# Turning x, y and seven heads' probabilities by transposing transfers in a two-block decoder kernel

## The reference, cut to what matters

```python
proj = rms_norm(h) @ w_in            # z, xbc, dt, q, k, v, two gates
xbc = silu(causal_depthwise_conv(xbc, conv_w, conv_b))
x, B, C = split(xbc)                 # x: 32 heads of 64, in 4 groups of 512 columns
# for each group: scores C.B * decay, applied to x*dt; state = B^T (x*dt*decay); y_off = C.state * decay
y = (y_diag + y_off + d_skip * x) * silu(z)
y = y * rsqrt(mean(y*y per group)) * ssd_norm
p = softmax over three dilated windows of q.k     # 8 heads
o = p @ v
merged = sigmoid(g_ssd) * (y @ w_ssd) + sigmoid(g_attn) * (o @ w_attn)
h = h + merged @ w_out ; h = h + (silu(gate) * up) @ w_down
```

## Time and profile before

| what | value |
|---|---|
| median of 3 runs | 1545.76 us (1545.64 to 1547.02) |
| the profiled execution's own time | 1546.51 us |
| its span, first to last instruction | 1544.7 us |
| busy: PE, DVE, ACT, POOL | 99%, 66%, 60%, 5% |
| granted TensorE clock, mean of the span | 1.000 |
| DMA queue of SP | 276.44 MB, 53.8% of 16 engines |

### The profile page before, as it was taken

How to read it: one execution, slowest core, us unless ns; L and a number is a source line. 1 busy time by engine, 2 the same in 40 slices (tenths; PEclk the granted TensorE clock), 3 DMA queues, 4 the chain that set the end, 5 groups by cost and what they waited for, 6 DMA issues and landing times.

```text
span 1544.7 us, 19149 instructions
## 1 busy us (share of the span) xinstructions
PE 1526.3 (99%) x7734; PEld 1288.4 (83%) x7734; DVE 1021.0 (66%) x1324; ACT 924.0 (60%) x1114; POOL 79.1 (5%) x55
## 2 busy tenths in 40 slices
PE   7999999999999999999999999999999999999998
PEld 7888888888888888988888888888888878888887
DVE  5978776646665554787886665566555576677665
ACT  5766777474355553667677566436555465656564
POOL 1000000000001000000000000000110020002000
PEclk9999999999999999999999999999999999999999
DMA  7455554554457675445555464446767575437541
GB/s 272 165 172 156 178 167 174 168 181 156 148 210 222 204 217 199 164 159 163 171 178 170 169 173 170 163 165 207 216 189 235 211 250 187 149 137 244 178 148 71
DMA packets 100399, 280.09 MB, mean 181 GB/s; under 512 B 65079, under 2 KB 66008, under 8 KB 69848
## 3 DMA queue, kind: packets, MB, share of 16 engines
q1 hardware_dynamic: 99208, 276.44, 53.8%
q10 hardware_dynamic: 1104, 2.43, 0.4%
HBM read 261.69 MB, written 1.84 MB: 171 GB/s over the span
## 4 chain that ended last, share of the span: by engine, by line
PE 86%; DVE 6%; ACT 4%; issue 3%; DMA 0%; ACTq 0%; DVEq 0%
PE ps L641 23%; PE ps L643 23%; PE ps L642 23%; PE ps L646 3%; DVE w_low L1640 2%; PE ps L911 2%; PE ps L912 2%; PE ps L913 2%; ACT w_high L1154 2%; PE ps L774 2%; DVE conv L1726 1%; DVE scratch L1931 1%; PE ps L818 1%; PE ps L749 0%; PE ps L779 0%
## 5 line engine op out<-in xcount | busy, mean ns | idle before, releaser
L1640 DVE TENSOR_TENSOR w_low<-w_raw,w_high 128x2048 fp32r<-128x2048 f32 (+1 forms) x250 | 566.7, 2267 | 410.1 <-ACT w_high L1154 343.3
L641 PE MATMUL ps<-w_high,u_high 128*128 128x512 f32 x1376 | 547.6, 398 | 0.5 <-DVE w_low L1640 0.5
L1154 ACT ACTIVATE w_high<-w_raw 128x2048 fp32r<-128x2048 f32 (+1 forms) x196 | 369.2, 1884 | 288.7 <-PE ps L643 275.3
L643 PE MATMUL ps<-w_high,u_low 128*128 128x512 f32 x1376 | 536.9, 390 | 0.0
L642 PE MATMUL ps<-w_low,u_high 128*128 128x512 f32 x1376 | 536.1, 390 | 0.0
L643 PEld LDWEIGHTS ps<-w_high,u_low 128*128 128x128 f32 x1376 | 258.2, 188 | 55.1
L641 PEld LDWEIGHTS ps<-w_high,u_high 128*128 128x128 f32 x1376 | 258.6, 188 | 54.6 <-issue 1.9
L642 PEld LDWEIGHTS ps<-w_low,u_high 128*128 128x128 f32 x1376 | 258.7, 188 | 53.0 <-issue 1.9
L641 PE MATMUL ps<-w_high,b_high 128*128 128x512 f32 x384 | 152.2, 396 | 0.0
L643 PE MATMUL ps<-w_high,b_low 128*128 128x512 f32 x384 | 149.8, 390 | 0.0
L642 PE MATMUL ps<-w_low,b_high 128*128 128x512 f32 x384 | 149.6, 390 | 0.0
(11 more groups left out here) (236 smaller groups left out, 1430.8 us busy)
## 6 DMA issues: line engine op xcount, KB each, us to landing
w_raw<-in_stream SPq DMA_DIRECT2D x238, 1024.0 KB, 4.9
w_raw<-in_stream SPq DMA_DIRECT2D x12, 512.0 KB, 4.1
par<-in_pars SPq DMA_DIRECT2D x4, 269.0 KB, 5.2
h<-in_x SPq DMA_DIRECT2D x4, 256.0 KB, 5.1
ple_gain<-in_ple_g ACTq DMA_DIRECT2D x2, 512.0 KB, 5.2
out<-h SPq DMA_DIRECT2D x4, 256.0 KB, 2.0
scratch<-in_const SPq DMA_DIRECT2D x1, 768.0 KB, 7.4
rev<-scratch ACTq DMA_DIRECT2D x1, 768.0 KB, 3.6
```

The lines of the kernel that those rows point to most:

```text
L641: nc.tensor.matmul(o, hi, whi, start=start, stop=False, **kw)
L643: return nc.tensor.matmul(o, lo, whi, start=False, stop=stop, **kw)
L1154: nc.scalar.activation(WH[:, c % RING, 0:n], W[:, c % RING, 0:n], ACT.Copy).then_inc(high_ready, 1)
L1640: return nc.vector.tensor_tensor(out=o, in0=a, in1=b, op=op)
```

## The change

x of each group, y of each group and the probabilities of heads 0 to 6 are no longer turned by PE. POOL splits the words, SP issues a transposing DMA and POOL (for q and k still ACT) puts them together. In each first-block layer this takes away 32 turns of x, 32 of y and 21 of probabilities, and adds 15 transposing DMAs on SP and some 30 copies on POOL. Slots move: DVE takes x in 2i+9 (was 2i+7), now from `xdt` in SBUF, y first, then `xds`, then `xdt` in place; the state's product moves from PE 2i+7 to 2i+8, behind the rows of that slot; ACT's copy of the state from 2i+8 to 2i+10; y is weighed in 2i+19 for groups 0 to 2 and 2i+16 for group 3 (was 2i+15); the product with v comes in s+4 (was s+3), its halves in s+6, its bank is 7 in place of 6; `QK_MERGE` of q2 goes from 30 to 31. SP's order within a slot is load, `turn_x`, `turn_qk`, `turn_y`, `turn_p`, rows.

```diff
+        X_TURN, QK_TURN, Y_TURN = (0, 2, 5, 8), (1, 4, 7, 10, 12, 13, 14), (3, 6, 9, 11)
+        QK_MERGE = (14, 24, 31, 34, 46, 47, 48)
+        X_AT = 9
+        Y_WEIGH = (19, 19, 19, 16)
+        O_AT = tuple(s + 6 - (s == 54) for s in HEAD_AT)
@@ SP
+            def turn_x(l, c):
+                for g, i in enumerate(XT):
+                    m = X_TURN[g]
+                    if c == 2 * i + 9:
+                        sp.wait_ge(words_split.sem, words_split.at(l, m + 1))
+                        sp.dma_start_transpose(x_back.rearrange("p (m r) -> p m r", r=P), ...)
+            def turn_y(l, c):          # c == 2 * i + 16
+            def turn_p(l, c):          # c == s + 6, heads 0 to 6
                     load(l * CHUNKS1 + c, c % RING, l * BLOCKS1 + c, 0, CH)
+                    turn_x(l, c)
                     turn_qk(l, c)
+                    turn_y(l, c)
+                    turn_p(l, c)
...
                     for g, i in enumerate(XT):
                         for t in range(T):
                             if c == (13 if g == 0 else 2 * i + 6 + 2 * t):
                                 load_rows(l, g, t)
@@ PE
-                    if c == 2 * i + 5:
-                        ... eight turns of conv
-                    if c == 2 * i + 13:
-                        ... eight turns of Y[g % 2]
-                    if c == 2 * i + 7:
-                        pe.wait_ge(xds_ready.sem, xds_ready.at(l, g + 1))
+                    if c == 2 * i + 8:
+                        pe.wait_ge(x_ready.sem, x_ready.at(l, 2 * g + 1))
...
+                        nc.tensor.matmul(ps[:, 5, :], btok[:, g, :], xds, start=True, stop=True).then_inc(state_ps.sem, 1)
+                    if n < 7 and c == s + 4:
+                        pe.wait_ge(pt_out.sem, pt_out.at(l, n + 1))
+                        if n == 6:
+                            pe.wait_ge(att_masked.sem, att_masked.at(l, 8))
+                        elif n:
+                            pe.wait_ge(o_ready.sem, o_ready.at(l, n))
+                        weigh_values(n)
@@ ACT
+                        if c == 2 * i + 10:
+                            ... copy of the state from ps[:, 5, :]
-                        if c == 2 * i + 15:
+                        if c == 2 * i + Y_WEIGH[g]:
                             for t in range(T):
                                 act.wait_ge(y_weighted.sem, y_weighted.at(l, 2 * g + t + 1))
...
@@ POOL, in this order
+                for g in range(GROUPS):
+                    split_x(g)
+                    if g:
+                        split_y(g - 1)
+                    else:
+                        split_qk(0)
+                    merge_x(g)
+                    if g:
+                        merge_y(g - 1)
+                        split_qk(g)
+                split_y(3)
+                merge_y(3)
+                ... lay_apart(n) and put_together(n) for heads 0 to 6, between them split_qk(4) to (6)
@@ DVE
+                        if c == 2 * i + X_AT:
+                            dve.wait_ge(x_whole.sem, x_whole.at(l, g + 1))
...
+                            tt(heads(xds), heads(xdt[:, 0, :]), ...).then_inc(x_ready.sem, 1)
+                        if c == 2 * i + Y_WEIGH[g]:
+                            dve.wait_ge(y_whole.sem, y_whole.at(l, g + 1))
```

More of the change, by code:

```diff
@@ L675, in ffn_turn, with weigh_values @@
                 last.then_inc(ffn_cols.sem, 1)
+            def weigh_values(n):
+                b, v = O_BANK[n], vv[n // 4][:, :, tok(n % 4)]
+                nc.tensor.matmul(ps[:, b, 0:S], v[:, 0], pT[:, 0:S], start=True, stop=False)
+                nc.tensor.matmul(ps[:, b, P:S], v[:, 1], pT[:, S:S + P], start=False, stop=True).then_inc(o_ps.sem, 1)
             def before(l, c):
@@ L751, in before @@
                             last.then_inc(row_ps.sem, 1)
-                    if c == 2 * i + 7:
-                        pe.wait_ge(xds_ready.sem, xds_ready.at(l, g + 1))
-                        pe.wait_ge(ssd_exp.sem, ssd_exp.at(l, 2 * g + 1))
-                        nc.tensor.matmul(ps[:, 6, :], btok[:, g, :], xds, start=True, stop=True).then_inc(state_ps.sem, 1)
-                for g, i in enumerate(XT):
-                    if c == 2 * i + 13:
-                        pe.wait_ge(y_scaled.sem, y_scaled.at(l, g + 1))
-                        if g < GROUPS - 1:
-                            pe.wait_ge(xdt_ready.sem, xdt_ready.at(l, g + 2))
-                        else:
[L762 to L766, removed]
+                    if c == 2 * i + 8:
+                        pe.wait_ge(x_ready.sem, x_ready.at(l, 2 * g + 1))
+                        if g == 0:
+                            pe.wait_ge(btok_out.sem, btok_out.at(l, 1))
+                            pe.wait_ge(cumt_out.sem, cumt_out.at(l, 1))
+                        else:
+                            pe.wait_ge(ssd_y.sem, ssd_y.at(l, 2 * g))
+                        nc.tensor.matmul(ps[:, 5, :], btok[:, g, :], xds, start=True, stop=True).then_inc(state_ps.sem, 1)
                 for g, i in enumerate(XT):
@@ new lines, in put_together, with split_x @@
+                def put_together(n):
+                    pool.wait_ge(p_turned.sem, p_turned.at(l, 16 * (n + 1)))
+                    if n:
+                        pool.wait_ge(o_ps.sem, o_ps.at(l, n))
+                    nc.gpsimd.tensor_copy(pT.bitcast(U16).rearrange("p (n h) -> p h n", h=2),
+                                          p_back[n // 4][:, :, :].rearrange("p (h k) n -> p h (k n)", h=2)).then_inc(pt_out.sem, 1)
+                def split_x(g):
+                    pool.wait_ge(conv_act.sem, conv_act.at(l, 3 + g))
+                    for t in range(T):
+                        ins = nc.gpsimd.tensor_copy(x_half[:, :, t], conv[:, :, tok(t)].bitcast(U16).rearrange("p j (n h) -> p h j n", h=2))
+                    ins.then_inc(words_split.sem, 1)
@@ L1877, in _ @@
                                 chain.then(dve, tt(dt_out, dt[:, 0:HEADS], dec_out, ALU.mult))
-                            tt(heads(xds), heads(ps[:, 4, :]), bc(dt_out[:, g * HPG:(g + 1) * HPG].unsqueeze(2), HPG, HD), ALU.mult)\
-                                .then_inc(xds_ready.sem, 1)
+                            for t in range(T):
+                                tt(heads(y[:, t, :]), heads(xdt[:, t, :]),
+                                   bc(par[:, C_DS + g * HPG:C_DS + (g + 1) * HPG].unsqueeze(2), HPG, HD), ALU.mult)
+                            tt(heads(xds), heads(xdt[:, 0, :]), bc(dt_out[:, g * HPG:(g + 1) * HPG].unsqueeze(2), HPG, HD), ALU.mult)\
+                                .then_inc(x_ready.sem, 1)
+                            for t in range(T):
+                                ins = tt(heads(xdt[:, t, :]), heads(xdt[:, t, :]),
+                                         bc(dt[:, t * HEADS + g * HPG:t * HEADS + (g + 1) * HPG].unsqueeze(2), HPG, HD), ALU.mult)
+                            ins.then_inc(x_ready.sem, 1)
                         for t, at_c in ((0, 2 * i + 8), (1, 2 * i + 10)):
```

192 lines of the change are left out of this document (121 added, 71 removed).

## The result

The changed kernel takes 1570.68 us (median of 4 runs, 1568.84 to 1571.85) against 1545.70 in the same session: ratio 1.0158, interval 1.0146 to 1.0170, **25 us slower where 12 were forecast** and 0.7 above the end of the range.

The account below looks back on a forecast made before the run. PE, busy 1526.3 of 1544.7 us, was taken to bound the kernel. Per layer -13.1 + 3.0 + 6.2 + 4.5 + 0.3 + 0.9 + 1.7 + 2.5 = +6.0, two +12.0 on 1545.8: 1558, range 1546 to 1570.

Parts of the forecast that it names:

- turns and waits for `pT` gone: On PE: turns of x, y and probabilities and seven waits for turned probabilities disappear; 13.1 us less a layer.
- New wait 1, rows: PE waits for group 0's rows, issued behind `turn_x` in SP's slot 13; 3.0 us a layer.
- New wait 2, group 2 (with `merge_y`): PE's state product waits for `xds` in slot 24: 6.2 us, plus 0.9 for `split_low` beside `merge_y`.
- New wait 2, group 3: PE's state product waits for `xds`, with y's weighing in slot 29 ahead of it; 4.5 us a layer.
- New wait 2, groups 0 and 1: PE's state product waits for `xds` with no weighing before it; 0.3 us for both groups.
- New wait 3, slot 47: PE's turns of q5 wait for bank 7 until head 3's halves are made in slot 48; 1.7 us a layer.
- Clock: PE's clock falls once a layer, after group 2's wait of 7 us; 2.5 us.
- the copy that meets DVE: Group 2's `split_low` on DVE falls beside `merge_y` on POOL; 0.9 us, bounds 0 and 1.9.
- more of the same: Rival: clock falls after other waits too, or POOL's copies stretch DVE's chain in several groups; 1563 to 1575, chance 0.13.
- Group 2's chain: ACT's and DVE's work from ACT's slot 23 to `xds`: 23.8 us against PE's 17.9.
- faster: Rival: in slots 23 and 29 ACT needn't wait for DVE, so state waits vanish; 1529.6 or 1524, chance 0.12.

Follow-up runs that it names:

- e9: The kernel before with only the probabilities' part of the change, and the halves of head 3 in slot 47 instead of 48; 1535.33 us.
- e10: As e9, with y also turned by transfers (weighed in 2i+17 for groups 0 to 2); x and the state's product as before the change; 1529.70 us.
- e1: The changed kernel, with POOL's joining copy of y taking only a sixteenth of its elements; 1560.02 us.
- e2: The changed kernel, with y of groups 0 to 2 weighed in slot 2i+17 instead of 2i+19; 1569.67 us.
- e4: The changed kernel, with group 0's two row transfers issued ahead of `turn_x` in SP's slot 13; 1564.36 us.
- the three moves: Edits to the changed kernel: state's product in slot 2i+9, group 0's row transfers ahead of `turn_x`, head 3's halves in slot 47; 1541.44 us.
- e5: The changed kernel, with POOL joining y in four instructions of a quarter each, every element joined; 1569.53 us.
- e3: The changed kernel, with PE's product for the state in slot 2i+9 instead of 2i+8; 1548.84 us.
- e6: The kernel before with the probabilities' part of the change alone; x, y and the state's product as before; 1539.67 us.
- e7: The changed kernel with the three moves; 1541.44 us.
- e12: The changed kernel with the three moves, and POOL joining y of group g-1 after it has split q; 1539.71 us.

## Why the prediction was wrong

Per layer, forecast against measured (mean of the two layers):

| step | forecast | measured |
|---|---|---|
| turns and waits for `pT` gone | -13.1 | -12.7 |
| New wait 1, rows | 3.0 | 1.6 |
| New wait 2, group 2 (with `merge_y`) | 7.1 | 6.5 |
| New wait 2, group 3 | 4.5 | 7.1 |
| New wait 2, groups 0 and 1 | 0.3 | 2.7 |
| New wait 3, slot 47 | 1.7 | 1.9 |
| Clock | 2.5 | 3.9 |
| sum | 6.0 | 11.0 |

The span gives 10.95 a layer; the first row's measured value is what the others leave of it.

- **What goes away** was right. From slot 36 to slot 60 the attention is 4.1 us shorter, 5.9 with the wait of slot 47 gone too (e9), where the forecast has 5.8. For y's four blocks in two layers 7.3 us were expected; e10 shows 4.7 in those layers, with four new waits at the turns of x set against the turns that are gone.
- **The step that failed is the one on the copy that meets DVE.** The prediction charged 0.9 us, once a layer, in group 2, and nothing in groups 1 and 3 ("the copies mostly fall into DVE's idle time" was the argument against the rival "more of the same"). The trace shows 2.2 to 2.3 in each of three groups. e1 takes the holds away: group 1's wait of 2.3 vanishes and group 3's is 4.9 (its distance 5.15 less 0.23), against the 4.5 forecast without a hold; in group 2, the one place that was charged, only 0.3 goes. The time falls by 10.7, where the forecast had 1.8 to give. The bound was wrong as well: it came from a splitting copy (1.89), and a joining one takes 2.6 alone and up to 3.50 when DVE holds it up first. The Trainium skill, "SBUF — State Buffer", section "Who interferes with whom", says that a VectorE instruction with two inputs in SBUF and a GpSimd instruction that reads SBUF exclude each other for a whole instruction. The trace agrees: 4.48 for 2.3, and 3.50 for 2.6 on POOL's side. The prediction had that rule in front of it, took the middle of its bounds, and asked the question for one group of three, the one in which the answer hardly counts.
- **The clock** was right in kind and wrong in count: five falls of 1.5 to 1.65 us (7.9) where two of 2.5 (5.0) were forecast. Once group 3 waits 7 us instead of 4.5 it is like group 2; but in e1, with 5.15 there, the clock still fell, so the forecast's count of one would have failed anyway. The Trainium skill, "TensorE: Matmul & The Clock Gate", section "Part 1: The HAM clock gate", says that idleness brings the low clock back; the granted 0.50 inside the wait agrees.
- **Group 2's chain** was right, not only its number. From the start of ACT's slot 23 to the end of slot 25's `split_high` the forecast had 15.4 + 4.2 = 19.6 us; the trace has 155.77 to 175.39, 19.6, with ACT idle for 2.96 us before the weighing's high halves. Without a hold the wait was to be 6.2, and e1 has 6.2 (6.41 less 0.23). What fails is the wish to save it there: e2 takes the weighing out and group 2 gains 0.3, because ACT then waits 1.85 us for DVE's gated y and POOL's copy meets a later operation. The rival "faster", priced at 12 in 100, rested on that place, and no run of x's part comes near it.
- **Rows**: the issue of x's transposing DMA was 3.56 us in the first layer, not the 5.34 of the earlier trace rows, so the wait was 1.6 and 1.5 and not 3.0. The place was right (e4).
- **Slot 47** was right to 0.2.

The errors partly cancel: groups 1 and 3 and the clock put 6.4 us a layer on top, rows and group 2 take 2.0 off. The larger cause, which the prediction only had in pieces: x's part does not pay. With probabilities, slot 47 and y the kernel takes 1529.70; with x too, and the three moves (slot 47 among them), 1541.44 (1.6 of it the fall in the second block; y is weighed two slots later there). x's part takes 7.3 us of turns from PE, where they covered DVE's lateness, and moves the work on x two slots towards its consumer, into a stretch where DVE has no room. That y and the probabilities pay is shown by e9 and e10, in the case of y less than its turns are worth; whether x could be turned by transfers with DVE's work spread otherwise wasn't tried.

## What to carry to other kernels

Work taken off the bounding engine is worth its time only as far as the engines behind it have room in that stretch: here the turns of probabilities and y were gain, and those of x a loss: more than the other two brought in the order of the change, and with the three moves still 12 us. When a copy goes to POOL, list every VectorE instruction that it can meet on the chain to the bounding engine in every group, and let each meeting cost up to the whole copy; then ask what else the chain waits for (in group 2 a hold of 2.3 us was worth 0.3). Cutting the copy into pieces didn't help here, putting the consumer's input ahead of it did. And a wait of PE can cost its clock on top: price each one with its fall, and don't count on the whole of a shortened wait while the clock still falls in it.

## What the runs showed of the hardware that was not expected

- DVE and POOL take turns instruction by instruction: a joining copy in four pieces held four DVE operations 0.4 to 0.5 us each, and lasted 6.38 us where one piece took 3.50 in the same place. The run's time is nearly that of one piece (e5: 1569.53 against 1570.68).
- An eight-column copy with a single input in SBUF is held like the big operations: 0.16 us became 2.48.
- A wait of the same length, 2.55 us in group 1, lowered the granted clock in the second layer and left it at 1.00 in the first. In e4 it was 2.54 and the clock held in both layers; in e5 it was 2.32 and the clock fell in both. The length alone doesn't decide; what does is open.
- The clock can fall without a wait. In the second block of e9 PE runs eight short products on 33 partitions, 2.84 us without a wait between them, and behind them the clock is low:
```profile
1229.33 2.84 PE L1033 MATMUL ps<-scratch 33*128 33x384 f32 x8
```
```profile
1232.00:1234.00 2.00, 2.00 (x6) 1.53 (x6) 0.18 (x2) 1.69 (x3) 0.00 (x0) 0.55 0.51 152
```
It costs 1.6 us. The same fall is in the profiled executions of e3, e6, e7 and e12; the same eight products run in the kernel before, at 1242 us, and in e10, and the clock holds. What decides is open. Comparisons between such kernels carry these 1.6 us.
- A shorter wait isn't a shorter time while the clock falls in it: in e2 the waits at the state's product lose 3.7 us and the falls cost 4.7 more (12.5 for 7.9). Behind every fall PE loses just under half of what it works at the low clock (1.5 of 3.1 us, 2.9 of 6.2 in e1).
- At the start of the kernel before, where the prediction read the lower clock out of products 0.21 us apart, the view of the granted clock says 1.00:
```profile
12.00:14.00 2.00, 2.00 (x11) 2.00 (x11) 0.51 (x1) 0.00 (x0) 0.00 (x0) 1.00 1.05 436
```
But the trace's first entry for the clock lies at 15.6 us, which is where the products change from 0.21 to 0.12 apart; before it there is no entry, and 1.00 is what the view prints then. So the record doesn't contradict the reading. The price of 2.5 was too high for the middle of the run because at the start PE worked through 5.7 us of slow products, and behind a wait through 3.1 to 3.4.
